# The column steps of a threshold search move from VectorE to GpSimd, and its counts one head later

## The reference, cut to what matters

```
# one layer over 1024 prompt frames and 64 sample frames, D_MODEL 1024
h    = rmsnorm(x, norm_g);  proj = h @ w_in        # two head groups side by side
# A) retention, 4 heads of 128, chunks of 64
# B) sparse attention, 8 heads of 64, 2 kv heads:
logits = relu(einsum('bqhd,bld->bqhl', qi, ki))    # 8 indexer heads of 64
index  = einsum('bqhl,bqh->bql', logits, wi)       # one row of scores per query
index  = where(admissible, index, -inf)            # own 64-chunk and all earlier ones
top_val, sel = top_k(index, 256)                   # at most 256 keys per query
p = softmax(q @ k[sel].T / 8);  o = p @ v[sel]
# gates, output projection, residual, final rmsnorm; keys, values, states are outputs too
```

## Time and profile before

| | |
|---|---|
| median of 3 runs | 928.48 us (925.73 to 930.24) |
| the profiled execution | 923.67 us, its span 922.1 us |
| PE busy | 803.6 us, 87% |
| DVE busy | 481.7 us, 52% |
| ACT busy | 334.1 us, 36% |
| POOL busy | 161.9 us, 18% |
| mean granted TensorE clock | 0.936 |

### The profile page before, as it was taken

The page is one execution under the profiler, slowest core; times in us unless marked ns, Lnnn a source line. Parts: engine busy times, 40 slices in busy tenths (PEclk is TensorE's granted clock), DMA queues, the critical chain, the costliest instruction groups (busy, mean ns, idle before and its releaser), DMA issues.

```text
span 922.1 us, 12271 instructions
## 1 busy us (share of the span) xinstructions
PE 803.6 (87%) x4185; PEld 674.2 (73%) x4185; DVE 481.7 (52%) x1179; ACT 334.1 (36%) x753; POOL 161.9 (18%) x352
## 2 busy tenths in 40 slices
PE   4788988998889899688699799999948999999984
PEld 3677877876768678677677588888837888888873
DVE  5433677778787878879625233333234533333322
ACT  5545555656456665567422111111034300000000
POOL 0323313131302122010022111112212000000000
PEclk9889979799999999799789799999978999999997
DMA  9412021202202020013263211111156433333321
GB/s 275 143 45 89 23 88 31 96 15 93 65 12 70 8 81 5 24 33 104 59 188 98 75 63 63 63 63 63 63 172 217 159 111 111 112 112 111 111 61 57
DMA packets 36462, 79.00 MB, mean 86 GB/s; under 512 B 7280, under 2 KB 9728, under 8 KB 35264
## 3 DMA queue, kind: packets, MB, share of 16 engines
q1 hardware_dynamic: 30112, 59.07, 20.5%
q0 software_dynamic: 6304, 19.36, 6.3%
HBM read 57.88 MB, written 20.53 MB: 85 GB/s over the span
## 4 chain that ended last, share of the span: by engine, by line
PE 54%; DVE 20%; issue 8%; DMA 7%; ACT 5%; POOL 3%; SPq 1%; DVEq 0%; POOLq 0%; ACTq 0%
PE bank L777 41%; DVE probs L1487 4%; DMA xT<-turned_x 3%; PE bank L891 3%; DVE work L1393 2%; DMA stage<-in_w_in 2%; PE bank L791 1%; DVE idx L1374 1%; DVE w_lo L1279 1%; DVE work L1428 1%; PE bank L837 1%; PE bank L880 1%; DVE top L1426 1%; PE bank L838 1%; PE bank L936 1%
## 5 line engine op out<-in xcount | busy, mean ns | idle before, releaser
L777 PE MATMUL bank<-w_hi,xT 128*128 128x512 f32 (+1 forms) x1152 | 379.2, 399 | 17.3 <-DMA xT<-turned_x 9.0
L777 PEld LDWEIGHTS bank<-w_hi,xT 128*128 128x128 f32 x1152 | 221.1, 195 | 68.1 <-DMA xT<-turned_x 12.8
L777 PE MATMUL bank<-w_lo,xT 128*128 128x512 f32 (+1 forms) x576 | 226.9, 394 | 0.0
L777 PEld LDWEIGHTS bank<-w_lo,xT 128*128 128x128 f32 x576 | 112.3, 195 | 19.4
L891 PE MATMUL bank<-v_sb,pT 128*128 128x64 f32 x648 | 91.9, 282 | 11.9 <-ACT pT L1124 11.5
L891 PEld LDWEIGHTS bank<-v_sb,pT 128*128 128x128 f32 x648 | 85.4, 202 | 19.6 <-ACT pT L1124 18.9
L880 PE MATMUL bank<-ident,probs 128*128 128x128 f32 x324 | 56.1, 286 | 17.4 <-ACT probs L1113 17.2
L1374 DVE SCALAR_TENSOR_TENSOR idx<-bank,iw_s,idx 128x384 f32<-128x384 f32 (+5 forms) x93 | 53.5, 611 | 32.3 <-ACT bank L1159 31.4
L1113 ACT ACTIVATE probs<-probs,low 128x128 f32<-128x128 f32 (+8 forms) x68 | 54.6, 803 | 42.1 <-DVE low L1487 42.0
L1124 ACT COPY pT<-bank 128x512 f32<-128x512 f32 (+3 forms) x104 | 48.8, 494 | 39.5 <-PE bank L880 38.6
L777 PE MATMUL bank<-w_hi,mT_hi 128*128 128x512 f32 x144 | 57.5, 399 | 2.6 <-DVE y_row L1663 2.6
(11 more groups left out here) (185 smaller groups left out, 1203.4 us busy)
## 6 DMA issues: line engine op xcount, KB each, us to landing
xT<-turned_x SPq DMA_DIRECT2D x36, 512.0 KB, 4.1
stage<-in_w_in SPq DMA_DIRECT2D x40, 256.0 KB, 3.1
turned_x<-xT SPq DMA_DIRECT2D x9, 1024.0 KB, 5.3
xin<-in_x_prompt SPq DMA_DIRECT2D x16, 256.0 KB, 3.9
early<-in_w_in SPq DMA_DIRECT2D x4, 1024.0 KB, 6.5
y_row<-in_x_prompt SPq DMA_DIRECT2D x16, 256.0 KB, 4.5
stage<-in_w_out SPq DMA_DIRECT2D x16, 256.0 KB, 3.4
out<-y_row POOLq DMA_DIRECT2D x8, 512.0 KB, 2.9
```

Of the source, the lines that this page charges most:

```text
L777: mm = pe.matmul(out, (lo if which == 2 else hi)[:, k, :], (w_lo if which == 1 else w_hi)[slot][:, k, 0:width], start=(i == 0), stop=(i == ...
```

## The change

DVE keeps only the counts. `search` becomes `count`, which waits for `guessed` or for POOL's last step (`refined`), counts and raises `counted`. The column steps become `refine` in POOL's queue, five times per searched tile; the reciprocal becomes a power of -1, and the window's bound and the 0.25 become constants in the instructions. The counts stand behind the heads 2 to 6 (`FIRST_COUNT = 2`) where they stood behind 1 to 5, and `keep` follows the last count behind head 6.

In POOL's queue the five `refine` stand behind the rotation of the next tile's `kv`. Its three stores, which stood ahead of the wait for the search, are now issued behind the last `refine`, and `partition_all_reduce` follows them.

```diff
+FIRST_COUNT = 2
-            def search(t, i):
+            def count(t, i):
                 n = keys_of(t)
...
                 if i == 0:
                     dve.wait_ge(guessed, no + 1)
                     if t != SAMPLE:
                         step(dve.memset(idx[0:CHUNK, n - CHUNK:n], MASKED))
-                now, was = counted(t, i)
-                step(dve.tensor_scalar(work[:, 0:n], idx[:, 0:n], above, None, ALU.is_gt, ALU.add, accum_out=seen))
-                step(dve.tensor_scalar(now, seen, -AIM, None, ALU.add))
...
-                if i:
-                    step(dve.scalar_tensor_tensor(out=gap, in0=was, scalar=0.25, in1=now,
-                                                  op0=ALU.add, op1=ALU.subtract))
-                    step(dve.reciprocal(gap, gap))
-                    step(dve.tensor_scalar(gap, gap, move, flattest, ALU.mult, ALU.max))
-                    step(dve.tensor_scalar(move, gap, steepest, now, ALU.min, ALU.mult))
                 else:
-                    step(dve.tensor_tensor(move, now, slope, ALU.mult))
-                step(dve.scalar_tensor_tensor(out=above, in0=move, scalar=far, in1=above,
-                                              op0=ALU.mult, op1=ALU.add))
+                    dve.wait_ge(refined, (COUNTS - 1) * no + i)
+                dve.tensor_scalar(work[:, 0:n], idx[:, 0:n], above, None, ALU.is_gt, ALU.add, accum_out=seen)\
+                   .then_inc(counted, 1)
...
-                        if 1 <= h <= COUNTS:
-                            search(t + 1, h - 1)
-                        if h == COUNTS + 1:
+                        if FIRST_COUNT <= h < FIRST_COUNT + COUNTS:
+                            count(t + 1, h - FIRST_COUNT)
+                        if h == FIRST_COUNT + COUNTS - 1:
                             keep(t + 1)
...
+            def refine(t, i):
+
+                pool.wait_ge(counted, COUNTS * search_no(t) + i + 1)
+                now, was = (over, over_was) if i % 2 == 0 else (over_was, over)
+                guess(pool.tensor_scalar(now, seen, -AIM, None, ALU.add))
+                if i == COUNTS - 1:
+                    guess(pool.tensor_scalar(far, now, now, ((WINDOW - 1) / 2) ** 2, ALU.mult, ALU.is_gt))
+                    return
+                guess(pool.tensor_scalar(far, now, now, ((WINDOW - 1) / 2) ** 2, ALU.mult, ALU.is_gt))
+                if i:
+                    guess(pool.tensor_scalar(gap, was, now, -0.25, ALU.subtract, ALU.subtract))
+                    guess(pool.tensor_tensor(gap, gap, cst[:, 11:12], ALU.pow))
+                    guess(pool.tensor_scalar(gap, gap, move, flattest, ALU.mult, ALU.max))
+                    guess(pool.tensor_scalar(move, gap, steepest, now, ALU.min, ALU.mult))
+                else:
+                    guess(pool.tensor_tensor(move, now, slope, ALU.mult))
+                pool.tensor_scalar(above, move, far, above, ALU.mult, ALU.add).then_inc(refined, 1)
+                pool.wait_ge(refined, (COUNTS - 1) * search_no(t) + i + 1)
...
                     rotate_iq(t + 1)
-                    rotate_kv(t + 1)
+                    kv_stores = rotate_kv(t + 1)
                 if t == SAMPLE:
                     rotate_aq(t)
                 if searched(t):
-                    pool.wait_ge(far_ready, no + 1)
+                    for i in range(COUNTS):
+                        refine(t, i)
+                if t + 1 < TILES:
+                    kv_stores()
+                if searched(t):
                     pool.partition_all_reduce(any_far, far, P, bass.bass_isa.ReduceOp.max).then_inc(any_ready, 1)
```

More of the change, by code:

```diff
@@ L163, in searched, with search_no @@
     return keys_of(t) > TOPK
+def search_no(t):
+    return len([x for x in range(t) if searched(x)])
 def normal_quantile(share):
@@ L200, in constants @@
     small[:, 0:4], small[:, 4:8] = to_end, to_end_s
-    small[:, 8], small[:, 9], small[:, 10] = -0.5, 0.5, ((WINDOW - 1) / 2) ** 2
+    small[:, 8], small[:, 9], small[:, 11] = -0.5, 0.5, -1.0
     small[:, 12:12 + WINDOW] = np.arange(WINDOW)
@@ L372, in hybrid_stream_step @@
         guessed = sem("guessed")
-        far_ready = sem("far_ready")
+        counted = sem("counted")
+        refined = sem("refined")
         any_ready = sem("any_ready")
@@ L1378, in add_index @@
                 wait_drained(dve, last_index(t))
-            def counted(t, i):
-                return (over, over_was) if i % 2 == 0 else (over_was, over)
-            def search(t, i):
+            def count(t, i):
                 n = keys_of(t)
-                no = t - len([x for x in range(TILES) if not searched(x)])
+                no = search_no(t)
                 if i == 0:
@@ L1391, in search @@
                         step(dve.memset(idx[0:CHUNK, n - CHUNK:n], MASKED))
-                now, was = counted(t, i)
-                step(dve.tensor_scalar(work[:, 0:n], idx[:, 0:n], above, None, ALU.is_gt, ALU.add, accum_out=seen))
-                step(dve.tensor_scalar(now, seen, -AIM, None, ALU.add))
[L1395 to L1400, removed]
-                if i:
-                    step(dve.scalar_tensor_tensor(out=gap, in0=was, scalar=0.25, in1=now,
-                                                  op0=ALU.add, op1=ALU.subtract))
-                    step(dve.reciprocal(gap, gap))
-                    step(dve.tensor_scalar(gap, gap, move, flattest, ALU.mult, ALU.max))
-                    step(dve.tensor_scalar(move, gap, steepest, now, ALU.min, ALU.mult))
-                else:
-                    step(dve.tensor_tensor(move, now, slope, ALU.mult))
-                step(dve.scalar_tensor_tensor(out=above, in0=move, scalar=far, in1=above,
-                                              op0=ALU.mult, op1=ALU.add))
+                else:
+                    dve.wait_ge(refined, (COUNTS - 1) * no + i)
+                dve.tensor_scalar(work[:, 0:n], idx[:, 0:n], above, None, ALU.is_gt, ALU.add, accum_out=seen)\
+                   .then_inc(counted, 1)
             def keep(t):
                 n = keys_of(t)
+                dve.wait_ge(counted, COUNTS * (search_no(t) + 1))
                 step(dve.memset(work[:, n:n + 8], TAKEN))
@@ L1436, in choose @@
                     return
-                dve.wait_ge(any_ready, t - len([x for x in range(TILES) if not searched(x)]) + 1)
+                dve.wait_ge(any_ready, search_no(t) + 1)
                 off = dve.value_load(any_far[0:1, :].bitcast(mybir.dt.int32))
@@ L1762, in rotate_kv, with store_kv @@
                 rows = slice(t * P, t * P + n) if t != SAMPLE else slice(0, DEC)
+                return lambda: store_kv(outs, rows, n, t)
+            def store_kv(outs, rows, n, t):
                 wait_drained(pool, ("kv", "A", t))
@@ L1802, in _ @@
             rotate_iq(0)
-            rotate_kv(0)
+            rotate_kv(0)()
             power_x(1)
```

## The result

| | before | after |
|---|---|---|
| median | 927.36 us (925.73 to 930.24) | 988.96 us (987.17 to 995.1) |
| ratio | | 1.0672, 95% interval 1.0615 to 1.073 |
| profiled execution, span | 923.67, 922.1 | 990.61, 989.0 |
| DVE busy | 481.7 | 444.7 |
| POOL busy | 161.9 | 228.4 |

61.6 us slower; the forecast was 45.5 slower, at 974, with a range of 950 to 1005. DVE lost 37 us of work and the program takes 62 us longer. The chain that ended last now reads as follows on the page; the earlier trace rows had DVE at 20% and POOL at 3%.

What follows compares the result with a forecast made beforehand. Waits by engine: PE 54%, DVE 20%, with DVE hardly resting in late searches. Delays from 9.6 us (tile 2) to 4.3 (tile 7) make 41.7, plus 3.8 in tile 8: 45.5 on 928.48 gives 974, range 950 to 1005.

Steps and rivals of the forecast that it cites:

- The late start: POOL's queue: all refinements stand behind the kv rotation, so count 1 waits; DVE idles about 6 us in tile 7's stage.
- R: End of the kv rotation on POOL, from which the refinements start; forecast at 358.03 in tile 7, 113.35 in tile 2.
- The round: DVE to POOL 0.2 us, seven POOL instructions 2.37, back 0.07: 2.64 us plus the count, three times after the first refinement.
- The forecast's high end: Column instructions on POOL as dear as the power, 0.65 us: 1.75 more a round, 6.3 a tile, up to 1018.
- The flag: POOL behind the last count: refinement 0.72, stores 2.13, library 6.15, flag 0.38 and 0.07; tile 2's bias 9.6 us late.
- The clock: PE's granted clock, 0.936 before, may drop as PE idles more; put at nothing, a reason the range reaches further up.
- What DVE gained: DVE loses column steps, 6.4 us a tile, 45 in all; none of it counts if DVE then waits for POOL.
- half is absorbed: Rival: PE's 31.5 us of slack and some of DVE's take up half of the shift: 951 us; 12%.
- The dear rival: Columns are dear on POOL, half way or more to 0.65 us an instruction: around 1005 us; 17%.
- the power of a negative number: Rival: POOL's power gives no number for a negative gap, searches take 32 rounds, 81 us a tile: 1300 us; 3%.

Runs made afterwards that it cites:

- the run with heads 1 to 5: Changed kernel with counts back behind heads 1 to 5 and two refinements ahead of the rotation (kv, in tile 8 aq): 952.66 us, 1.0294 of the kernel before.

## Why the prediction was right, and where it was short

**The late start: right.** Forecast for tile 7's stage: DVE idles about 6 us ahead of count 1. It did for 6.75. R was forecast at 358.0 on the clock of the kernel before; measured 407.86, less the 49.4 us by which the stage began later, 358.5. The first refinement to the count took 1.50 (407.86 to 409.36) for 1.27. Moving two refinements ahead took 26 us off.

**The round: right in kind, the term mis-sized.** This is the largest part of what the forecast was short, 16 us between the medians and 20 in the profiled executions. I had 2.64 us and the count, 3.96 in tile 7. Measured 4.56, in tile 2 3.9 for 3.29. The crossings were as forecast or shorter: 0.17 from DVE to POOL (410.64 to 410.81), 0.04 back (413.88 to 413.92). The steps were not. With one column as a scalar they took 0.29 to 0.31 and followed each other at 0.39, with two 0.34 to 0.38, at 0.48; I had taken 0.30 for all from rows with constants. 0.6 us a round, three rounds, seven tiles: 12.6 us. The forecast's high end covered it. By the Trainium skill ("GPSIMD Engine Reference", Performance versus the Vector engine) and its factor of two, which it gives for 2048 elements, the round's steps were estimated at 3.3 and the time at 997; measured were 3.07 and 989. So the rule was nearer than the row I chose. That is partly luck: the seven steps together took 3.07 for VectorE's 1.66, 1.85 times, but the power alone (0.57) is 3.5 times VectorE's reciprocal (0.16), and a step with two columns as scalars (0.37) 1.4 times VectorE's (0.27).

**The flag: right, and read late.** The end of the flag behind the end of tile 2's last count: forecast 9.4, measured 9.15 (127.68 to 136.83), in tile 7 10.04 (424.29 to 434.33). That reading it costs nothing was wrong. Between its end and `bias` lie 0.92 us in tile 2 and 0.65 in tile 7 (434.33 to 434.98). VectorE waited for it in tiles 2 to 5, 8.6 us in all, and 2.9 of them lie between the flag's end and `bias` (0.92, 0.67, 0.65 and 0.65). In tiles 6 and 7 the flag came at the same time as the turned keys, and VectorE idled 0.07 and 0.19 us. So the reading cost some 3 us in all; I had bounded it at 2.

**The clock: left at nothing, and not nothing.** The same matmuls took 29.5 us more of PE. Busy time and granted clock of the phase in the kernel before, then in the changed one:

```profile
85.00:475.00 390.00, 335.44 (x1953) 288.63 (x1954) 295.43 (x768) 227.01 (x487) 75.96 (x211) 0.92 0.17 54
```

```profile
85.00:540.00 455.00, 364.92 (x1947) 316.07 (x1948) 258.23 (x578) 229.79 (x487) 142.34 (x400) 0.82 0.15 47
```

Most of it lies where PE waits anyhow. In tile 8's stage it does not. Ahead of the `aq` projection the clock was 1.00 before (from 397 on), and now:

```profile
452.00:458.00 6.00, 3.69 (x18) 3.33 (x17) 1.88 (x6) 4.50 (x9) 2.70 (x11) 0.68 0.00 0
458.00:464.00 6.00, 6.00 (x34) 5.34 (x35) 3.71 (x8) 3.06 (x8) 0.00 (x0) 0.75 0.00 0
```

There the rotation ends 36.0 us after the stage's start, before 33.9: 2.1 us, which is nearly half of what tile 8 lies above its forecast. The rest there is the longer round, and two rounds of 4.99 us: DVE had a weight to split between counts, a pass with two inputs from SBUF (L1286, 474.68 to 475.43), and the first column step beside it took 0.58 us for 0.23 (474.92 to 475.50). In the other stages the lower clock did not delay the start of the chain. Counted from the start of its stage, the end of the guess comes 0.8 us later in the sum of all seven stages, and the end of the `kv` rotation 2.6 us earlier in the sum of tiles 2 to 7. No run here held the clock still, so the share of the clock in the 62 us is read from the profile and not shown by an experiment.

**What DVE gained: nothing, as said.** PE's waits for the exponential, of the kernel before in 85 to 475 us, then of the changed one in 85 to 510:

```profile
PE bank L880 <- ACT probs L1113: 16.9, 18, 2.3
```

```profile
PE bank L887 <- ACT probs L1120: 48.2, 24, 4.0
```

What DVE had free went into waits on the other side. The second window leaves out most of the last attention; up to 540 us, where the same work ends, the row reads 49.5, so PE waited 33 us more. The rival "half is absorbed" fell; the shifts went through undiminished and a little grown. The dear rival fell too, but not by much: the steps of a round took 0.70 us more than I had (3.07 for 2.37), where it began at half of 1.75, that is 0.88. No search took the long way with 32 rounds, so the power of a negative number was sound.

**A step that held by luck.** I put nothing down for the later head. In the changed kernel that holds, since count 1 waits longer for the rotation than the first count is late. Alone it costs 15 us.

In sum, from the runs: the column steps' place with what follows them costs 26 us (the run with heads 1 to 5), the rotation still ahead of the third refinement among it. The rotation ahead of the first two and the later head, which belong together in this queue, cost 36 (988.96 less 952.66).

## What to carry to other kernels

Taking work off a busy engine gains nothing if the work sits in a loop between its own instructions: what counts is the latency of the round trip, and what stands ahead of the helper's part in its queue.
